# Second attention of a two-block transformer kernel: values held stationary, branches on column halves, weights scaled by GpSimd

## The reference, cut to what matters

```python
p_c = masked_softmax(s_c, cmp_end[None, :] <= t[:, None])    # 15 compressed keys
o_c = jnp.einsum('bghqn,bngd->bqghd', p_c, vc)
p_s = masked_softmax(s_s, valid_s[:, :, None])               # selected keys
o_s = jnp.einsum('bghqk,bgqkd->bqghd', p_s, v_g)
p_w = masked_softmax(s_w, valid_w)                           # window
o_w = jnp.einsum('bghqk,bkgd->bqghd', p_w, vw)
out = gb[..., 0:1] * o_c + gb[..., 1:2] * o_s + gb[..., 2:3] * o_w
...
return o @ w_out
```

## Time and profile before

| | us |
|---|---|
| median of three runs | 907.17 |
| span of the profiled execution | 906.0 |
| TensorE busy in it | 888.7 (98%) |
| VectorE busy | 645.3 (71%) |
| ScalarE busy | 509.7 (56%) |
| GpSimd busy | 124.6 (14%) |
| second attention, from `turn_p(1, 0)` to the end of the last `turn_outputs` | 378.70 to 438.46 |

### The profile page before, as it was taken

How to read it: one execution, slowest core, us unless ns; L and a number is a source line. 1 busy time by engine, 2 the same in 40 slices (tenths; PEclk the granted TensorE clock), 3 DMA queues, 4 the chain that set the end, 5 groups by cost and what they waited for, 6 DMA issues and landing times. The chain is left out here.

```text
span 906.0 us, 14857 instructions
## 1 busy us (share of the span) xinstructions
PE 888.7 (98%) x4796; PEld 743.3 (82%) x4796; DVE 645.3 (71%) x1305; ACT 509.7 (56%) x1017; POOL 124.6 (14%) x168
## 2 busy tenths in 40 slices
PE   8999999999999999999999999999999999999998
PEld 7878787888888888888878888888887778878876
DVE  4768756766666679787467666666876878777785
ACT  6653836445444456686354444444656666666573
POOL 1310300000000000355010000000530401400401
PEclk9999999999999999999999999999999999999999
DMA  9643143656555557101437665555464445454431
GB/s 336 226 150 114 31 157 116 209 191 197 193 188 197 193 186 232 48 25 48 140 116 223 195 189 192 198 185 191 142 221 144 140 140 184 149 179 141 163 116 47
DMA packets 41609, 145.75 MB, mean 161 GB/s; under 512 B 4688, under 2 KB 6224, under 8 KB 41552
## 3 DMA queue, kind: packets, MB, share of 16 engines
q1 hardware_dynamic: 41264, 144.93, 48.2%
q10 hardware_dynamic: 288, 0.07, 0.0%
HBM read 143.93 MB, written 1.05 MB: 160 GB/s over the span
## 5 line engine op out<-in xcount | busy, mean ns | idle before, releaser
L463 DVE TENSOR_TENSOR wl<-raw,wh 128x1024 fp32r<-128x1024 f32 (+2 forms) x270 | 329.3, 1223 | 89.7 <-ACT wh L458 87.0
L458 ACT ACTIVATE wh<-raw 128x1024 fp32r<-128x1024 f32 (+2 forms) x270 | 281.7, 1046 | 66.0 <-PE acc L355 43.3
L353 PE MATMUL acc<-wh,xhl 128*128 128x512 f32 (+1 forms) x472 | 190.8, 404 | 1.3 <-DVE wl L463 0.9
L355 PE MATMUL acc<-wh,xhl 128*128 128x512 f32 (+1 forms) x472 | 184.6, 391 | 0.0
L354 PE MATMUL acc<-wl,xhl 128*128 128x512 f32 (+1 forms) x472 | 184.0, 390 | 0.0
L353 PEld LDWEIGHTS acc<-wh,xhl 128*128 128x128 f32 x472 | 88.7, 188 | 25.8 <-issue 8.0
L355 PEld LDWEIGHTS acc<-wh,xhl 128*128 128x128 f32 x472 | 88.6, 188 | 19.1
L354 PEld LDWEIGHTS acc<-wl,xhl 128*128 128x128 f32 x472 | 88.9, 188 | 16.3
L353 PE MATMUL acc<-wh,hh 128*128 128x512 f32 x256 | 100.2, 392 | 0.0
L354 PE MATMUL acc<-wl,hh 128*128 128x512 f32 x256 | 100.0, 391 | 0.0
L355 PE MATMUL acc<-wh,hl 128*128 128x512 f32 x256 | 99.7, 390 | 0.0
(11 more groups left out here) (302 smaller groups left out, 1350.5 us busy)
## 6 DMA issues: line engine op xcount, KB each, us to landing
raw<-stream SPq DMA_DIRECT2D x266, 512.0 KB, 3.4
raw<-stream SPq DMA_DIRECT2D x4, 352.0 KB, 6.5
h<-x SPq DMA_DIRECT2D x4, 256.0 KB, 4.0
out<-h SPq DMA_DIRECT2D x3, 256.0 KB, 2.1
row<-rows SPq DMA_DIRECT2D x1, 700.0 KB, 9.4
probs<-sel SPq DMA_DIRECT2D x1, 512.0 KB, 8.3
cst<-consts SPq DMA_DIRECT2D x1, 507.0 KB, 7.6
out<-h SPq DMA_DIRECT2D x2, 128.0 KB, 2.0
```

The lines of the kernel that those rows point to most:

```text
L353: nc.tensor.matmul(out_, ah, bh, start=start, stop=False, skip_group_check=True)
L355: return nc.tensor.matmul(out_, al, bh, start=False, stop=stop_, skip_group_check=True)
L458: nc.scalar.activation(used(u, wh[:, u % SPLIT, :]), used(u, raw[:, u % RAW, :]), ACT.Copy).then_inc(w_hi, 1)
L463: nc.vector.tensor_tensor(used(u, wl[:, u % SPLIT, :]), used(u, raw[:, u % RAW, :]), used(u, wh[:, u % SPLIT, :]).bitcast(F32), ALU.subtra ...
```

## The change

- The weights are scaled before they are turned. GpSimd no longer computes the reciprocal; VectorE does (`inverted`, RECIPROCAL, `s_coef`). GpSimd multiplies it with the gate and then scales the weights of both branches in `probs` in two instructions of 256 and 512 elements per partition (`weighed`, signalling `s_weighed`). `turn_p` of both branches now waits for `s_weighed`, which comes after the exponentials.
- `c_mix` replaces `mix`: values (128x64) stationary, turned weights moving, 256 and 128 columns. Branch 0 writes partitions 0 to 63 of `misc` and branch 1 partitions 64 to 127, that is, the two halves of the array's columns. Four matmuls of two passes stand where six stood.
- VectorE copies the 128x256 result as it is (`c_kept`) to `o_tok` or `Y`. `c_scaled` and the addition on GpSimd are gone.
- `turn_outputs` adds both halves with `fold` (128x64, two identities one above the other, a new constant): per pair of heads two matmuls of 256 moving columns onto two column halves, where two of 128 columns with the identity stood.

```diff
@@ turn_p
-                pe.wait_ge(s_exped, 2 * st + a + 1)
+                if st < STEPS_AB:
+                    pe.wait_ge(s_exped, 2 * st + a + 1)
+                else:
+                    pe.wait_ge(s_weighed, T * (st - STEPS_AB + 1))
@@ TensorE, values
+            def c_mix(n):
+                st, d0 = STEPS_AB + n, HD * (n % CG)
+                pe.wait_ge(s_copied, 2 * st + 2)
+                pe.wait_ge(s_scaled, st)
+                for c in range(2):
+                    cols = (2 - c) * P
+                    for a in range(2):
+                        v0 = (CVS, CVW)[a] + d0
+                        last = mm(misc[a * HD:(a + 1) * HD, c * P:SEQ], Y[:, c, v0:v0 + HD],
+                                  c_pt(st, a)[:, c * SEQ:c * SEQ + cols], start=c == 0, stop=c == 1,
+                                  skip_group_check=True)
+                last.then_inc(s_mixed, 1)
@@ turn_outputs
-                    for t in range(T):
-                        last = mm(bank[:, t * P:(t + 1) * P], o_tok[:, t, j * P:(j + 1) * P], ident,
-                                  start=False, stop=True, skip_group_check=True)
+                    for a in range(2):
+                        last = mm(bank[a * HD:(a + 1) * HD, :], fold, c_out(2 * j + a), start=False, stop=True,
+                                  skip_group_check=True)
@@ GpSimd
+            def weighed(st, coef):
+                for t in range(T):
+                    n = (t + 1) * P
+                    pb = probs[:, st % DEEP, t * 2 * P:t * 2 * P + 2 * n].rearrange("p (a k) -> p a k", a=2)
+                    g.tensor_tensor(pb, pb, c_stat(coef, st)[:, :, t:t + 1].broadcast_to([P, 2, n]),
+                                    ALU.mult).then_inc(s_weighed, 1)
...
-                if it < STEPS_C:
-                    s_ = STEPS_AB + it
-                    pc_.link(coefficients(s_))
...
+                s_ = STEPS_AB + it
+                pool.wait_ge(s_coef, s_ + 1)
+                pc_.link(g.tensor_tensor(c_stat(cf, s_), c_stat(rs, s_),
+                                         gate_t[:, :, 1:3, it].rearrange("p t b -> p b t"), ALU.mult))
+                weighed(s_, cf)
@@ VectorE
+            def inverted(st):
+                dve.wait_ge(s_exped, 2 * st + 2)
+                v_.reciprocal(c_stat(rs, st), c_stat(su, st)).then_inc(s_coef, 1)
+
+            def c_kept(n):
+                dve.wait_ge(s_mixed, STEPS_AB + n + 1)
+                v_.tensor_copy(c_out(n), misc[:, 0:SEQ]).then_inc(s_scaled, 1)
...
+                if 0 <= it - 2 < STEPS_C:
+                    inverted(STEPS_AB + it - 2)
+                if it >= STEPS_C:
+                    c_kept(it - DEEP - 2)
                 if 0 <= it - DEEP < STEPS_C:
                     p_second(STEPS_AB + it - DEEP)
-                if it < STEPS_C - 1:
+                if it < STEPS_C:
                     peaks(STEPS_AB + it)
-                if it > DEEP:
-                    c_scaled(it - DEEP - 1)
-                if it == STEPS_C - 1:
-                    peaks(STEPS_AB + it)
+                if DEEP + 2 <= it < STEPS_C:
+                    c_kept(it - DEEP - 2)
```

## The result

The changed kernel takes **951.87 us** (median of four runs, 948.72 to 953.60) against 907.11 us (four runs, 906.90 to 907.47). The ratio is 1.0482, 95% interval 1.047 to 1.0495. So it is slower, as forecast, and inside the range of 929 to 952, but only just: two of the four runs lie above its end, and the point forecast of 935.5 was 16.4 us too low. The profiled execution took 952.18 us with a span of 950.3, which is 44.3 more than the 906.0 of before.

The account below looks back on a forecast made before the run. TensorE (busy 98% of the span) was taken to bound the kernel, VectorE nearly full too. 906.0 + 4.7 (start) + 19.3 (loop) + 4.4 (end) = 934.4; the median lies 1.2 above, so 935.5 us, range 929 to 952.

Parts of the forecast that it names:

- The text's own case: Whole kernel: copy waits on TensorE, column halves side by side, clock at 1.00; 935.5 us, range 929 to 940, chance 0.62.
- the rival of halves in turn: Mixes and folds: column halves run one after the other, a mix takes 1.50 instead of 0.86; 949 us, chance 0.25.
- the clock: Second attention: clock stays at 1.00; rival: falls to 1.2 GHz, up to 26 us more, about 960, chance 0.08.
- The loop: Iterations 5 to 15: mix waits for VectorE's copy, second turn to mix 2.71 instead of 0.35 us; period 4.77, section +19.3.
- The mix: `c_mix`: column halves run side by side and it takes 0.86 us where the old mix took 1.29.
- The start: Up to `turn_p(1, 0)`: turns wait for GpSimd's weights, so it stands at 383.4 instead of 378.70, +4.7 us.
- The end: Iteration 16 to projection: four mixes save 1.7, folds cost 2.4, waits in iterations 17 and 18 cost 3.8; +4.4 us.
- GpSimd "no cost": After the start: GpSimd needs 2.0 us of a 4.8 us period, two iterations ahead of its turn, so costs nothing.
- The rival "not slower": Second attention: `c_mix` finds its bank read in time, twelve iterations take 35.5 instead of 39.5 us; 908.6, chance 0.05.

Follow-up runs that it names:

- before_late: The kernel before, with only its scaling read out of `misc` one iteration later, where `c_kept` stands in the changed kernel: 959.08 us, ratio 1.0561.
- kept_old_place: The changed kernel with the copy `c_kept` put back where the scaling of the kernel before stood, one iteration earlier: 919.95 us, ratio 1.0135.
- kept_first: The changed kernel with `c_kept` first in VectorE's iteration, ahead of `p_second` and `peaks`, also for iterations 5 to 15: 921.05 us, ratio 1.0159.
- filled: The changed kernel with idle multiplications of zeros in TensorE's waits ahead of `c_mix` in iterations 5 to 15, and 18 in iteration 3: 936.94 us, ratio 1.032.
- one_half: kept_old_place with both branches accumulated on the same column half, so the passes of `c_mix` run one after the other: 921.82 us, ratio 1.0159.
- inv_early: kept_old_place with the reciprocal `inverted` one iteration earlier, behind the peaks and ahead of VectorE's copy of `misc` and extra work: 916.34 us, ratio 1.01.

## Why the prediction was right, and where its size failed

- **The number: right by luck.** The text's own case had a range of 929 to 940, and the time is 12 us above its end. The wider range reached 952 only because it took in the rival of halves in turn at 949, and that rival fell. What filled the gap was the clock, which the range was meant to leave out.
- **The loop: right.** The wait is there in iterations 5 to 15, released by the copy, and it is the order alone that makes it: before_late has it without any other part of the change, kept_old_place and kept_first do not have it. Its length was forecast at 2.71 from second turn to mix and measured at 2.70 in filled.
- **The mix: right.** 0.86 taken, 0.81 measured at full clock (the switch ahead of it is 0.44 instead of the 0.35 taken, so that both together are nearly as forecast). The rival of halves in turn fell: one_half measures what it would have been, 1.44 against the 1.50 of the text.
- **The clock: the step that failed.** The text held that the clock stays at 1.00, because it did in a stretch where TensorE was busy 2.81 of 4 us, and gave its fall a chance of 0.08. It was 0.65 on average from 384 to 454 and 0.50 at times. The rival's price was "up to 26" (its own 2.4 us per iteration would have given 12 x 2.4 = 29); it was 15, the distance from filled to the changed kernel. The stretch of the earlier trace rows stands at the kernel's very start, once and for 4 us. It bears nothing on a pattern of 2.2 us of standing still that comes back eleven times. The right reading would have been to give the case at full clock, 935, and the case at half clock, up to 960, like weight: whoever forecasts a closed loop on TensorE forecasts its idle time too. The Trainium skill, TensorE: Matmul & The Clock Gate, section Why this matters for your kernels, warns of idle gaps between bursts. The fall agrees with that in kind, but the gaps that brought it here, 2.18 us, are shorter than those the section warns of.
- **The loop and the clock add up.** Half a clock does not stretch the wait as such (2.19 us in iteration 5, whose turn still took 0.52, and 2.18 behind the turns of 0.84; VectorE's work fills it). It stretches what surrounds it: turns and scores from 1.20 to 1.99 us (444.95 to 446.94), second turn to mix from 2.70 to 3.02, mix from 0.81 to 1.48. That makes 6.49 instead of 4.72 in an iteration that is at half clock throughout.
- **The start: right.** +5.1 for +4.7, by the chain that the text names. Its own terms add up to 383.2, or +4.5, and not to the 383.4 that it states. GpSimd's pair takes 1.61 us where 1.74 was worked out, but ScalarE's exponentials begin at 379.61 instead of 379.24, because at half clock its copy begins 0.94 us after the turn instead of 0.56. From first turn to `turn_p(1, 0)` filled, with its clock at 0.97 from 379 to 384, took 383.58 - 378.58 = 5.00 us, and the changed kernel, at 0.50, took 383.77 - 378.29 = 5.48. So about 0.5 us of the start is the clock.
- **The end: right in sum.** Each call of `turn_outputs` went from 422.50 - 420.39 = 2.11 to 462.89 - 460.18 = 2.71 us, +0.60 for two folds and +2.4 for all eight, as forecast. The fold itself occupies 0.58; most of the rest comes on the product behind it, 0.63 where the same product took 422.06 - 421.62 = 0.44 before. The two waits of iterations 17 and 18 were smaller than forecast (mixes at 1.98 and 1.92 instead of 2.3). At full clock the end is +3.8 (filled); the missing 0.6 was made up in the changed kernel by the last turns and the mix of iteration 16 at half clock.
- **GpSimd "no cost": right for a period of 4.8, wrong for the pace of before.** In the changed kernel TensorE waits for GpSimd only once, at the start. In the kernels without the loop it is the next thing that TensorE waits for. The rival "not slower" at 908.6 is thereby too low in its own terms: its condition was met in kept_old_place and inv_early, and they stand at 920 and 916.

What is left of the change without the loop, from inv_early (span 913.9, +7.9): +4.3 at the start, where the first turns wait for the GpSimd link; +2.9 in the middle (42.35 for 39.50 us), where the mixes are shorter but TensorE waits for GpSimd and, for 3.1 us, for VectorE; +0.6 at the end, where folds eat what the mixes save. None of the versions tried is faster than the kernel before.

Open: how much of inv_early's middle is port contention and how much the GpSimd link itself, since no kernel moved VectorE's weight rests out of the way. Also open is why the clock, under the same wait in each iteration, changes to and fro: 0.77, 0.71 and 0.50 in the three shorter stretches above, 0.76 again from 420 to 425 and from 430 to 435, 0.50 from 440 to 450. That it falls for the waits is shown by filled, when it falls is not explained.

## What to carry to other kernels

Where two engines hand a buffer back and forth, look at which instruction the release stands behind. A read that is moved behind a wait on the very engine that will need the buffer turns an overlap into a relay, and one instruction's place then costs more than all the matmuls it serves. If TensorE would stand still in such a relay again and again, price the stage at half clock as well as at full, and test it with idle matmuls that do nothing but keep it busy. Work that is taken off a full engine and put on an idle one is free only if nobody waits for its result; here TensorE waited 11.1 us for it as soon as the loop was gone.

## What the runs showed of the hardware

- **Column halves** run side by side for float32 also where each takes in all 128 partitions: eight passes (four of 256, four of 128 columns) occupy 0.81 us on two halves, 1.44 on one.
- **The clock** fell to 0.50 with TensorE idle 2.2 us in each iteration of 5.4 to 8.1 us, though not in every one of them, and also after one wait of 2.68 us at the start. It fell behind waits of 1.91 us (filled, 384 to 389: 0.69) and 1.84 us (kept_old_place, whose turn at 414.07 lasts 0.87 instead of 0.55), but not behind one of 1.87 us in inv_early, whose turn at 410.25 lasts 0.52. In kept_old_place it also fell at 400.47, with no wait over 0.94 us in the 10 us before. So the length of one wait does not tell it. It was back at 1.00 in the end of the stage (464 to 469 us) with waits of 1.4 us still there. Work that leads nowhere in these waits made the kernel 15 us faster, with the clock at 1.00 from 388 to 438.
- **GpSimd and VectorE** hinder each other: two products took 2.55 instead of 1.61 us beside a weight rest with two SBUF inputs, and a VectorE scalar step on 32 elements took 1.07 instead of 0.18 us beside GpSimd's products. Both are read from rows, not tested by a run.
